# Attention over two parities of heads: tile 1's steps take two heads of one parity, and VectorE scales a step's weights ahead of the fill's splits

## The reference

```python
    s = einsum('bhgqd,bhkd->bhgqk', q, k) * HEAD_DIM ** -0.5
    p = masked_softmax(s, mask)                       # float32, over the keys
    o = einsum('bhgqk,bhkd->bhgqd', p, v)
    o_all = sum over branches of sigmoid(gate) * o    # then o @ w_attn_out
```

## Time and profile before

| | |
|---|---|
| Time, median of 3 runs | 775.38 us (774.64 to 776.61) |
| The profiled execution: time | 775.23 us |
| its span in the profile | 773.5 us |
| TensorE matmul busy | 755.1 us, 98% |
| VectorE busy | 526.3 us, 68% |
| ScalarE busy | 421.4 us, 54% |

### The profile page before, as it was taken

The page is one execution under the profiler, slowest core; times in us unless marked ns, Lnnn a source line. Parts: engine busy times, 40 slices in busy tenths (PEclk is TensorE's granted clock), DMA queues, the critical chain, the costliest instruction groups (busy, mean ns, idle before and its releaser), DMA issues.

```text
span 773.5 us, 12562 instructions
## 1 busy us (share of the span) xinstructions
PE 755.1 (98%) x5029; PEld 668.7 (86%) x5029; DVE 526.3 (68%) x868; ACT 421.4 (54%) x801; POOL 67.5 (9%) x95
## 2 busy tenths in 40 slices
PE   8999999999999999999999999999899999999998
PEld 7999988889899988888888889988678888888886
DVE  4767576786665767876467757588887777447762
ACT  5366555456554546565356547577546656345640
POOL 7200000001011000100000005403300000000000
PEclk9999999999999999999999999999999999999999
DMA  7988545335335556566556563833344655665521
GB/s 240 297 275 266 122 79 177 110 114 159 111 113 187 172 182 209 173 218 208 176 175 204 167 188 109 278 131 109 109 140 134 199 185 203 197 195 164 196 77 54
DMA packets 108286, 131.52 MB, mean 170 GB/s; under 512 B 4269, under 2 KB 97515, under 8 KB 108228
## 3 DMA queue, kind: packets, MB, share of 16 engines
q1 hardware_dynamic: 105780, 126.04, 51.4%
q0 software_dynamic: 2160, 4.16, 2.3%
q10 hardware_dynamic: 288, 0.52, 0.2%
HBM read 128.87 MB, written 1.84 MB: 169 GB/s over the span
## 4 chain that ended last, share of the span: by engine, by line
PE 76%; DVE 13%; ACT 6%; issue 4%; POOL 1%; DMA 0%; SPq 0%; ACTq 0%; DVEq 0%; POOLq 0%
PE B L1478 24%; PE B L1455 21%; PE B L1439 14%; PE B L1460 11%; DVE LO L922 4%; ACT HI L522 2%; ACT PR L632 1%; DVE SM L1041 1%; PE B L1665 1%; PE B L1536 1%; DVE PR L1062 1%; PE B L1618 1%; PE B L1628 1%; PE B L1485 1%; POOL SGC L472 1%
## 5 line engine op out<-in xcount | busy, mean ns | idle before, releaser
L922 DVE TENSOR_TENSOR LO<-RAW,HI 128x1024 fp32r<-128x1024 f32 x240 | 283.0, 1214 | 150.4 <-ACT HI L522 150.0
L522 ACT ACTIVATE HI<-RAW 128x1024 fp32r<-128x1024 f32 x240 | 237.9, 1040 | 56.7 <-PE B L1478 55.4
L1455 PE MATMUL B<-AA,HI 128*128 128x512 f32 x704 | 243.4, 398 | 0.5 <-DVE AA L928 0.5
L1478 PE MATMUL B<-HI,AA 128*128 128x512 f32 (+1 forms) x800 | 210.3, 348 | 3.9 <-DVE AA L1372 3.8
L1460 PE MATMUL B<-AA,LO 128*128 128x256 f32 x704 | 183.2, 281 | 0.0
L1439 PE MATMUL B<-AA,HI 128*128 128x256 f32 (+1 forms) x960 | 177.8, 287 | 1.0 <-ACT KT L552 1.0
L1478 PEld LDWEIGHTS B<-HI,AA 128*128 128x128 f32 x800 | 140.8, 189 | 23.6 <-DVE AA L1372 4.2
L1439 PEld LDWEIGHTS B<-AA,HI 128*128 128x128 f32 (+1 forms) x960 | 149.2, 191 | 5.9 <-issue 2.9
L1455 PEld LDWEIGHTS B<-AA,HI 128*128 128x128 f32 x704 | 126.7, 188 | 25.2 <-issue 1.1
L1460 PEld LDWEIGHTS B<-AA,LO 128*128 128x128 f32 x704 | 132.9, 189 | 8.2
L1478 PE MATMUL B<-LO,AA 128*128 128x512 f32 (+1 forms) x400 | 138.7, 347 | 0.0
(11 more groups left out here) (286 smaller groups left out, 626.4 us busy)
## 6 DMA issues: line engine op xcount, KB each, us to landing
RAW<-in_w_in SPq DMA_DIRECT2D x29, 1024.0 KB, 5.6
RAW<-in_w_gate SPq DMA_DIRECT2D x22, 1024.0 KB, 5.4
RAW<-in_w_up SPq DMA_DIRECT2D x22, 1024.0 KB, 5.4
RAW<-in_w_down SPq DMA_DIRECT2D x22, 1024.0 KB, 5.0
RAW<-in_w_in SPq DMA_DIRECT2D x11, 512.0 KB, 6.8
RAW<-in_w_attn_out SPq DMA_DIRECT2D x4, 1024.0 KB, 5.4
RAW<-in_w_o SPq DMA_DIRECT2D x4, 1024.0 KB, 5.0
RAW<-in_w_out SPq DMA_DIRECT2D x4, 1024.0 KB, 5.2
```

Of the source, the lines that this page charges most:

```text
L522: e.activation(pieces(HI, NSPL, i, k), pieces(RAW, NRAW, i, k), ACT.Copy).then_inc(split_hi, 1)
L922: e.tensor_tensor(pieces(LO, NSPL, i, k), pieces(RAW, NRAW, i, k), pieces(HI, NSPL, i, k), ALU.subtract).then_inc(split_lo, 1)
L1455: return e.matmul(dst[:, :], hi[:, t, c0:c0 + 128], flatten(AA[:, ch + t, :, :]), start=(t == 0), stop=(t == nk - 1))
L1478: x = e.matmul(dst, a, w[:, t, c0:c0 + n], start=(first and t == 0 and k == 0), stop=(last and t == nk - 1 and k == 2))
```

## The change

Three parts.

- The list of steps: in tile 1 a step had heads h0 and h0 + 1 with h0 = 0 or 2; now h0 is 0 or 1, and the step has heads h0 and h0 + 2, of one parity. The numbers of steps and their order by g stay. The scores and the gates take the heads with that step of 2.
- The output products: in tile 1 a step had four products of 128 columns (two blocks of keys by two parities). It now has two of 256 columns, one for each block of keys, each for both heads. Tile 0's two products stay as they are. The flags that begin and end an accumulation follow; the compressed products of tile 1's second round move from its first to its third step.
- VectorE's loop: weights(i) stands directly behind most(i), ahead of the fill.

```diff
--- before.py
+++ after.py
@@ -271,7 +271,7 @@
 
 
         def in_round(c, t, br):
-            return [(br, 2 * c + half, t, h0) for h0 in range(0, 4, 4 // (t + 1)) for half in range(2)]
+            return [(br, 2 * c + half, t, h0) for h0 in range(t + 1) for half in range(2)]
 
         steps, ends = [], []
         for t in range(2):
@@ -1046,7 +1046,7 @@
                 k, q = s % 2, s % 3
                 br, g, t, h0 = steps[s]
                 n = 16 if br is None else 4 // (t + 1)
-                gate = GATE[:, t, 0, :] if br is None else GATE[:, t, 1 + br, 4 * g + h0:4 * g + h0 + n]
+                gate = GATE[:, t, 0, :] if br is None else GATE[:, t, 1 + br, 4 * g + h0:4 * g + 4:t + 1]
                 pr = PR[:, k, :].rearrange("p (h n) -> p h n", h=n)
                 den, cf = SM[:, 3 * q + 1, 0:n], SM[:, 3 * q + 2, 0:n]
                 e.wait_ge(exp_sb, s + 1)
@@ -1127,10 +1127,9 @@
             for i in range(NSTEP + 2):
                 if i < NSTEP:
                     most(i)
+                    weights(i)
                 for _ in range(FILL_AT[i]):
                     next(filler)
-                if i < NSTEP:
-                    weights(i)
                 if i - 2 in ends:
                     taken(ends.index(i - 2))
             for _ in filler:
@@ -1615,7 +1614,7 @@
                 for j in range(n):
                     for m in range(2):
                         r = slice(64 * m, 64 * m + 64)
-                        e.matmul(sc[m][:, j, :], QT[r, c, h0 + j, t * 128:t * 128 + 128], KT[r, br, c, 0:w],
+                        e.matmul(sc[m][:, j, :], QT[r, c, h0 + (t + 1) * j, t * 128:t * 128 + 128], KT[r, br, c, 0:w],
                                  start=(j == 0), stop=False)
                 for m in range(2):
                     x = e.matmul(sc[m][:, :, w - 128:w], identb[:, :], mask, start=False, stop=True)
@@ -1633,8 +1632,8 @@
 
                 k = s % 2
                 br, g, t, h0 = steps[s]
-                first, last = s == 0 or s - 1 in ends, s in ends
-                if first:
+                at = s - max([0] + [end + 1 for end in ends if end < s])
+                if at == 0:
                     take(7, turn_lo, 5 + (0 if s == 0 else ends.index(s - 1) + 1))
                 e.wait_ge(pturn_sb, s + 1)
 
@@ -1652,18 +1651,14 @@
                     return
                 e.wait_ge(vals_sb, 2 * br + 2)
                 blocks = PT[:, k, :].rearrange("p (b a q) -> p a b q", a=2, q=128)
-                for kb in range(t + 1):
-                    for odd in range(2):
-                        r = slice(64 * odd, 64 * odd + 64)
-                        v = VV[:, br, kb, 64 * g:64 * g + 64]
-                        if t == 0:
-                            o, w = 256 * (g % 2), blocks[:, odd]
-                            dst = OB[r, o:o + 256].rearrange("p (b q) -> p b q", b=2)
-                        else:
-                            o, w = 256 * (g % 2) + 64 * h0, PT[:, k, 256 * odd + 128 * kb:256 * odd + 128 * kb + 128]
-                            dst = OB[r, o:o + 128]
-                        x = e.matmul(dst, v, w, start=first and kb == 0, stop=last and kb == t)
-                if first and g >= 2:
+                o = 256 * (g % 2)
+
+                for a in range(2):
+                    odd, kb = (a, 0) if t == 0 else (h0, a)
+                    x = e.matmul(OB[64 * odd:64 * odd + 64, o:o + 256].rearrange("p (b q) -> p b q", b=2),
+                                 VV[:, br, kb, 64 * g:64 * g + 64], blocks[:, a], start=at == 2 * h0 and kb == 0,
+                                 stop=s + 2 * (t - h0) in ends and kb == t)
+                if at == 2 * t and g >= 2:
                     x = compressed(1)
                 x.then_inc(o_pe, 1)
```

## The result

| | before | after |
|---|---|---|
| Time, median | 775.55 us (774.64 to 776.61, 4 runs) | 784.87 us (784.4 to 786.05, 4 runs) |
| Ratio | | 1.0124, 95% interval 1.0112 to 1.0136 |
| Profiled execution: time | 775.23 us | 785.32 us |
| its span | 773.5 us | 783.6 us |

The account below looks back on a forecast made before the run. TensorE was taken as the bound, its attention losses reaching the kernel's end nearly whole. 775.23 + 6.7 (products) + 1.7 (VectorE's order) = 783.6, stated as 783.7 us; 8-in-10 range 779.4 to 786.3.

Parts of the forecast that it names:

- The first term: TensorE's output products in tile 1: both of a step's products land on one half, +6.7 us over 16 steps.
- The second: VectorE's new order in the attention: new waits of TensorE +4.2 against -2.5 for stalls gone, +1.7 us.
- a third, the clock: Half-clock stretch of 3.4 us at 523.5 us: it need not return in the same place, 1.7 us either way.
- The price of the products: One step of tile 1 on TensorE: 1.01 us after the change where it took 0.59, 0.42 more.
- The rival of the other side: Tile 1's output products: four 256-column passes take 0.58 us wherever they land; 772.9, or 777.1 with new waits; chance 0.07.
- VectorE's order: VectorE's loop with weights ahead of splits and drains: stalls for weights go, TensorE waits for later drains; +1.7 us.
- All three places that I named: TensorE's new waits for VectorE's drains from iterations 7 (1.6 us), 11 (1.3) and 20 (1.3).
- L1628 no longer waits: -2.5 us: TensorE's turning of the weights, three stalls before 171 us: weights come earlier, so the stalls go, -2.5 us.
- The third size: Iteration 20, convolution's output product: drain L1117 ends at 200.1, TensorE wants it at 198.8, a wait of 1.3 us.
- Sum of the new waits: TensorE's waits behind VectorE's drains from iterations 7, 11 and 20, together +4.2 us.
- Only TensorE's part is real: Rival on the attention: drains come in time and stalls go, so only the products cost; 779.6 us, chance 0.17.
- VectorE becomes the bound: Rival on iterations 0 to 15: VectorE's longer cycle bounds TensorE; 786 us or more, chance 0.13.

Follow-up runs that it names:

- two runs on the halves: New steps, old VectorE order, tile 1's second product on the other half: 0.9995; kernel before, both parities on one half in 12 of 16 steps: 1.0075.
- steps_two_halves: Kernel after with VectorE's old loop, and in tile 1 each step's second product on the other 64 PSUM rows; 775.28 us, ratio to before 0.9995.
- early_where_idle: Kernel before with weights ahead of the fill only in eight iterations where VectorE's first split waits for ScalarE; 773.90 us, ratio to before 0.9981.
- order_only: Kernel before with VectorE's new loop, weights ahead of the fill, old steps and products; 778.14 us, ratio to before 1.0029.
- order_but_7_20: Kernel before with weights ahead of the fill, except in iterations 7 and 20, where they stand behind it; 774.79 us, ratio to before 0.9995.
- steps_only: Kernel after with VectorE's old loop: new list of steps and output products, weights behind the fill; 781.74 us, ratio to before 1.0071.

## Why the prediction was right

**The whole.** 783.7 us forecast, 784.87 measured; +8.4 forecast, +9.3 by the medians. The first term was right in size and cause. The second came out near its size in part by luck, and a third, the clock, was only named.

**The price of the products** was right to its last digit: 1.01 us a step forecast, 1.01 measured, and +6.7 us for 16. It followed from seeing that `odd` no longer alternates. The two runs on the halves show it as the cause, not only the sum as fitting. The rival of the other side (passes cost what tile 0's cost) had its condition at 0.75 us a step; it fell with 1.01. The rule of the Trainium skill, "TensorE: Matmul & The Clock Gate", Part 3, that different column groups run at once, agrees with the steps of every run here: 0.59 us on two halves, 1.01 and 1.02 on one. The 60 cycles a matmul of "TensorEngine Tiling (Array Packing)", Instruction Overhead, do not show: 64 records fewer, with both halves in use, changed the time by -0.2 us in the attention (steps_two_halves), where the estimate by that page was -1.6.

**VectorE's order** came out at +1.4 us where I said +1.7, but not in the way that I said. All three places that I named have their wait. Two are a third of what I gave them: 0.51 for 1.6 behind L1102 in iteration 8 and 0.47 for 1.3 in iteration 12. The third has 1.20 for 1.3. The step that failed is "L1628 no longer waits: -2.5 us". TensorE did not get those microseconds: right behind the turning stand the first outputs of a new round, and before they write to bank B7 VectorE must have taken the finished round's low part (L1068). That started at 124.01 us, where it had started at 123.84. Of the stall of 1.02 us at step 6, 0.82 moved by one instruction, and of the 1.05 at step 9, 0.86 reappeared one step later. I had listed what stands behind the weights on VectorE, but not what TensorE meets next once it is early. Late by such a wait, it met the drains later and waited less there. At iteration 8 VectorE kept my time (L1102 began at 129.22, I had 129.1), but TensorE, which I had asking at 127.9, asked at 129.19: 0.82 us by the wait at L1658, and 0.45 since the attention began that much later in this execution. At iteration 12 it asked at 152.68 where I had 151.7. The third size was nearly met, although my own terms made it larger than I wrote: the third block before begins at 197.78, with 0.84 that is 198.6, and the wait 1.5 and not 1.3. Sum of the new waits: 4.2 forecast, 3.9 measured. That these agree is luck: the three named waits came to 2.2, which is 2.0 less than forecast, and two that I had not named came to 1.7.

**The rest** is 1.3 us between the attention's 8.0 and the medians' 9.3, and 2.1 in the profiled executions. There it is the start (0.45) and the clock (1.6). I named the clock as good for 1.7 us either way, taking the 3.4 us at half clock before for a loss of half their length. That step was wrong: the stretch before costs nothing. early_where_idle has no such stretch in its profiled execution (mean granted clock 1.00 from 500 to 760 us), and its lead over the kernel before is 2.55 us ahead of the place (last pass of the output products at 233.35 against 235.90) and 2.56 behind it:

```profile
500.00:760.00 260.00, 250.34 (x1496) 215.89 (x1496) 185.95 (x318) 144.68 (x269) 15.19 (x20) 1.00 0.47 152
...
556.27 0.47 PE L1481 MATMUL B<-HI,AA 128*128 128x512 f32 x1 [2.23 <-DVE AA L1375]
```

(558.83 for the same product before.) So the clock could only add to the time here, and it did where the low stretch fell on dense products. That it accounts for the rest of the medians too is likely and was not measured; the interval of their ratio is about 0.9 us to either side.

**Chances.** Slower by more than 0.3% had 0.92 and happened. *Only TensorE's part is real* fell with the waits of order_only; *VectorE becomes the bound* fell with order_but_7_20, where two iterations took the whole loss away.

## What to carry to other kernels

A product with 64 output rows fills half the array, so what counts is which half its neighbour takes: order products to alternate between PSUM rows 0 to 63 and 64 to 127; whether they had 128 or 256 columns made no difference here. Where an instruction is moved ahead in a list, the engines that wait for what it now stands before pay for it; here the move paid when made only in iterations where the engine idles anyway. And where a stall goes, look at the next wait of the engine that is freed: here 1.7 of 2.5 us stood there again, for something that the stall had hidden. And a stretch at half clock costs what stands in it: nothing at 523.5 us before, 1.6 us at 568.5 after.

## What was unexpected of the hardware

Matmuls on different halves need not start in the order of the kernel's text. In the kernel after, step 20's two products (L1658, upper half) stand ahead of the eight compressed products (L1644, alternating halves, lower first). On the timeline of that step they interleave:

```profile
216.58 0.43 PE L1658 MATMUL B<-PT,VV 128*64 128x256 f32 x1
216.59 0.43 PE L1644 MATMUL B<-TMP,SGA 128*64 128x128 f32 x2
216.84 0.59 PE L1658 MATMUL B<-PT,VV 128*64 128x256 f32 x2
217.07 0.43 PE L1644 MATMUL B<-TMP,SGA 128*64 128x128 f32 x2
217.28 0.38 PE L1658 MATMUL B<-PT,VV 128*64 128x256 f32 x1
```

The first compressed product starts 0.01 us after L1658's first pass and 0.25 before its second. So the free half takes up a later product while the other works on an earlier one. In steps_only the same step interleaves in the same way, from 215.07 us on. It saves nothing here: step and compressed products take 218.46 - 216.58 = 1.88 us. Before they took 1.46 together (201.19 to 202.65, at step 18), and with one plain step beside each the sums are 2.89 and 2.05, twice 0.42 apart as everywhere. That the chip chooses this order, and not the compiled list, is read from the starts alone.

The granted clock falls to half for 3 to 7 us once in the second block in eight of the nine profiled executions, for example at 523.5 us in the kernel before, at 526.8 in order_only and at 568.5 in the kernel after. In that of early_where_idle it does not. TensorE had been busy for 1.59 of 3.40, 4.90 of 6.70 and 4.99 of 8.40 us ahead of it. Which of the gaps of that stage it follows was not settled.
